# Two groups of the state-space stages at a time in the halves of TensorE's columns, and gate rows spread by DMA, in a two-layer hybrid backbone step

## The reference, cut to what matters

```python
def _adaln(cond, w, b):
    m = jax.nn.silu(cond) @ w + b          # w is 1024 x 3072
    return jnp.split(m[:, None, :], 3, axis=-1)     # shift, scale, gate

def _layer(x, mods, lp, ...):
    shift, scale, gate = mods
    h = _rmsnorm(x, lp['norm_g']) * (1.0 + scale) + shift
    z = h @ lp['w_in']                      # one projection feeds three mixers
    ...
    ya = _conformer_conv(conv_in, ...)      # A: depthwise conv, 31 taps, LayerNorm, silu
    yb = _s5_bidirectional(ssm_in, ...)     # B: 32 groups x 16 channels, 64 complex states
    o = _blocked_attention(q, k_all, v_all) # C: 8 heads, 2 KV heads, RMS-normed q and k
    ...
    mixed = g_a * br_a + g_b * br_b + g_c * br_c
    x = x + gate * (mixed @ lp['w_out'])
```

## Time and profile before

| | us |
|---|---|
| median of 3 runs | 691.57 |
| profiled execution | 691.89 |
| its span | 690.1 |
| PE busy | 643.8 (93%) |
| DVE busy | 535.7 (78%) |
| ACT busy | 309.6 (45%) |
| POOL busy | 80.4 (12%) |

### The profile page before, as it was taken

How to read it: one execution, slowest core, us unless ns; L and a number is a source line. 1 busy time by engine, 2 the same in 40 slices (tenths; PEclk the granted TensorE clock), 3 DMA queues, 4 the chain that set the end, 5 groups by cost and what they waited for, 6 DMA issues and landing times.

```text
span 690.1 us, 9683 instructions
## 1 busy us (share of the span) xinstructions
PE 643.8 (93%) x3573; PEld 460.7 (67%) x3573; DVE 535.7 (78%) x996; ACT 309.6 (45%) x534; POOL 80.4 (12%) x81
## 2 busy tenths in 40 slices
PE   3699799998999999999999899999999999989997
PEld 1377674554745688877887587465565578878885
DVE  2669889996676967789966837999767799987663
ACT  2665350540545354444546636044256544445441
POOL 2100220147000000010001710012700000010000
PEclk9999999999999999999999999999999999999999
DMA  7991817654583655655443337570443345655531
GB/s 263 373 315 58 264 60 230 238 186 119 174 284 120 180 160 173 183 162 153 162 149 113 116 137 267 179 258 29 151 151 106 106 127 184 199 163 181 184 102 61
DMA packets 67307, 117.66 MB, mean 171 GB/s; under 512 B 11052, under 2 KB 15484, under 8 KB 67260
## 3 DMA queue, kind: packets, MB, share of 16 engines
q1 hardware_dynamic: 66980, 116.94, 52.9%
q10 hardware_dynamic: 280, 0.11, 0.1%
HBM read 112.51 MB, written 1.38 MB: 165 GB/s over the span
## 4 chain that ended last, share of the span: by engine, by line
PE 72%; DVE 12%; SPq 6%; ACT 3%; issue 3%; DMA 2%; POOL 1%; ACTq 0%; POOLq 0%; DVEq 0%
PE proj L816 19%; PE proj L844 11%; PE proj L846 11%; PE proj L845 11%; PE side L831 4%; PE side L987 3%; PE side L974 2%; PE side L1068 2%; DVE raw_split L1506 2%; PE long L786 2%; PE side L1016 2%; SPq L629 1%; PE proj L786 1%; PE side L1066 1%; DMA raw<-in_w_in 1%
## 5 line engine op out<-in xcount | busy, mean ns | idle before, releaser
L816 PE MATMUL proj<-raw,hT 128*128 128x512 f32 (+1 forms) x320 | 132.0, 558 | 0.0
L1609 DVE SCALAR_TENSOR_TENSOR cvacc<-cvpad,taps,cvacc 128x256 f32<-128x256 f32 x240 | 99.0, 478 | 0.2
L816 PEld LDWEIGHTS proj<-raw,hT 128*128 128x128 f32 x320 | 58.2, 190 | 58.8 <-issue 57.0
L1212 ACT ACTIVATE wide_split<-raw 128x1024 fp32r<-128x1024 f32 x56 | 58.7, 1060 | 56.2 <-PE proj L846 56.2
L1506 DVE TENSOR_TENSOR raw_split<-raw,wide_split 128x1024 fp32r<-128x1024 f32 x56 | 67.8, 1221 | 17.2 <-ACT wide_split L1212 16.5
L845 PE MATMUL proj<-raw_split,H_split 128*128 128x512 f32 x192 | 75.5, 393 | 0.0
L844 PE MATMUL proj<-wide_split,H_split 128*128 128x512 f32 x144 | 57.9, 402 | 4.2 <-DVE raw_split L1506 4.2
L846 PE MATMUL proj<-wide_split,H_split 128*128 128x512 f32 x144 | 56.9, 395 | 0.0
L1212 ACT ACTIVATE utok_split<-raw 128x1024 fp32r<-128x1024 f32 x28 | 29.6, 1058 | 34.5 <-PE proj L846 34.5
L1506 DVE TENSOR_TENSOR raw_split<-raw,utok_split 128x1024 fp32r<-128x1024 f32 x28 | 34.2, 1221 | 12.3 <-ACT utok_split L1212 12.3
L2010 POOL TENSOR_SCALAR st<-st 128x1 f32<-128x1 f32 x8 | 4.6, 571 | 332.5 <-DVE st L1924 251.8
(11 more groups left out here) (255 smaller groups left out, 1377.6 us busy)
## 6 DMA issues: line engine op xcount, KB each, us to landing
raw<-in_w_in SPq DMA_DIRECT2D x104, 512.0 KB, 4.5
raw<-in_w_ada SPq DMA_DIRECT2D x48, 512.0 KB, 5.4
raw<-in_w_out SPq DMA_DIRECT2D x16, 512.0 KB, 3.8
raw<-in_w_ssm_glu SPq DMA_DIRECT2D x8, 512.0 KB, 7.1
raw<-in_w_ssm_out SPq DMA_DIRECT2D x8, 512.0 KB, 3.8
raw<-in_w_attn_out SPq DMA_DIRECT2D x8, 512.0 KB, 4.2
raw<-in_w_conv_out SPq DMA_DIRECT2D x8, 512.0 KB, 3.7
raw<-in_w_in SPq DMA_DIRECT2D x8, 256.0 KB, 3.6
```

The costliest lines, as they stand in the source:

```text
L816: m = T.matmul(proj.bank((l, u, s))[:, 0:n], lhs[:, s, kt, :], w[:, i, :], start=(kt == 0), stop=last)
L1212: S.activation(piece_room[m], piece_raw(m), ACT.Copy).then_inc(piece_hi, 1)
L1609: m = V.scalar_tensor_tensor(acc, src, taps[:, t, j:j + 1], acc, ALU.mult, ALU.add)
```

## The change

Five parts.

1. **K in pairs.** Groups g and g + 4 go alternately into output partitions 0 to 47 and 64 to 111, that is into the two halves of the array's columns, in 4 banks of 8 groups instead of 8 of 4. K 0 now stands ahead of unit kv, K 1 ahead of unit sg. ACT makes as many copies as before, four per bank.
2. **Y in pairs.** Group 4q + i and group 16 + 4q + i go alternately into partitions 0 to 63 and 64 to 127. ACT copies out 64 x 256 twice per quarter instead of 64 x 512 once.
3. **States.** All four quarters are copied right after the scan, quarters 2 and 3 into `tA` and `tB`, which are free then.
4. **Gates.** The PE matmuls of L1103, their ACT copies, the transposes `adaT` 2 and the bias addition on DVE go. In their place SP loads the gate's bias into rows of `taprow` at unit q (two DMAs, `bias_loads`), POOL adds it to the adaLN rows into `bz` after K 1 (`gaterow`, 128 x 256), and SP's `gate_rows`, ahead of the fourth slab of each wout, issues four DMAs of 128 KB: each reads one row of 256 numbers (1 KB) of one partition of `bz` 128 times and writes it to all 128 partitions of `th`. DVE waits for them (`gate_in`).
5. **Taps.** Ahead of Y 22 and 12 (layer 0 and 1) instead of 26 and 14; in Y 12 instead of 19; in B0 and B1 14 or 20 each instead of 12 or 18; what is left, at C0, is 20 and 24 instead of 13 and 19.

```diff
-TAPS_IN_ZONE = (26, 14)
-TAPS_IN_Y = (8, 5, 6)
+TAPS_IN_ZONE = (22, 12)
+TAPS_IN_Y = 12
-CONV_B = (12, 18)
+CONV_B = (14, 20)
...
+            + [("UT",), ("S",), ("cp",), ("bz", 0), ("convT", 0), ("convT", 1), ("unit", "q"), ("K", 0), ("unit", "kv"), ("bz", 1),
+               ("adaE", l, 2), ("sumsq", 0), ("sumsq", 1), ("K", 1), ("gaterow",), ("unit", "sg"), ("scan", 0, NCHUNK),
+               ("HY",), ("unit", "ag")] + nxt("adaE", n, 0)
+            + [("qkn",), ("conv", TAPS_IN_ZONE[l], None), ("Y",)] + nxt("adaT", n, 0)
...
+        states = [HY[:, 0], HY[:, 1]] + [t[:, :].rearrange("p (g r s k) -> p g r s k", g=8, r=2, s=NS) for t in (tA, tB)]
...
+            def gate_rows(l, h):
+                sp.wait_ge(gaterow_done, l + 1)
+                for s in range(NS):
+                    key = (l, "gate" + str(h), s)
+                    th_claim(sp, key)
+                    for i in range(2):
+                        row = P // ADA_TILES * (2 * h + i) + s
+                        sp.dma_start(th_view(key)[:, ADA_W * i:ADA_W * i + ADA_W],
+                                     gaterow[row:row + 1, :].unsqueeze(1).to_broadcast([1, P, ADA_W])).then_inc(gate_in, 16)
...
+                    if stg[0] == "wout" and i == 3:
+                        gate_rows(l, stg[1])
...
                         for b in range(4):
-                            g = 4 * i + b
                             for r in range(2):
-                                m = T.matmul(side.bank(key)[0:48, 80 * b:80 * b + 80], bz[:, r, g % 16, :],
-                                             CP[:, r, :, g, :], start=(r == 0), stop=(r == 1))
+                                for a in range(2):
+                                    g = 8 * i + 4 * a + b
+                                    m = T.matmul(side.bank(key)[64 * a:64 * a + 48, 80 * b:80 * b + 80], bz[:, r, g % 16, :],
+                                                 CP[:, r, :, g, :], start=(r == 0), stop=(r == 1))
...
-                        for gi in range(8):
-                            g = 8 * q + gi
-                            o = side.bank(key)[0:64, 64 * gi:64 * gi + 64]
-                            T.matmul(o, Uz[:, g, :], M[:, :, g // 2, :], start=True, stop=False)
+                        for i in range(4):
+                            gs = [4 * q + i, G // 2 + 4 * q + i]
+                            out = [side.bank(key)[64 * a:64 * a + 64, 64 * i:64 * i + 64] for a in range(2)]
+                            for a in range(2):
+                                T.matmul(out[a], Uz[:, gs[a], :], M[:, :, gs[a] // 2, :], start=True, stop=False)
                             for r in range(2):
-                                m = T.matmul(o, HY[:, q % 2, gi, r, :, :].rearrange("p s k -> p (s k)"),
-                                             CP[:, r, 1:L + 1, g, :], start=False, stop=(r == 1))
+                                for a in range(2):
+                                    m = T.matmul(out[a], states[q][:, 4 * a + i, r, :, :].rearrange("p s k -> p (s k)"),
+                                                 CP[:, r, 1:L + 1, gs[a], :], start=False, stop=(r == 1))
...
-                if k == "wout":
-                    h = stg[1]
-                    side.drained(pe, ("adaT", l, 2))
...
+                elif k == "gaterow":
...
+                    tt_(gaterow, adarow[part], biasrow, ALU.add).then_inc(gaterow_done, 1)
```

More of the change, by code:

```diff
@@ L192, in side_uses @@
     if k == "K":
-        return [(("K", l, 4 * stage[1] + i), 1) for i in range(4)]
+        return [(("K", l, 2 * stage[1] + i), 1) for i in range(2)]
     if k == "att":
@@ L213, in side_uses @@
     if k == "wout":
-        merged = [(("mixT", l, s, 1), 1) for s in range(NS)] if stage[1] == 0 else []
-        return [(("gate", l, stage[1], s), 1) for s in range(NS)] + merged
+        return [(("mixT", l, s, 1), 1) for s in range(NS)] if stage[1] == 0 else []
     return []
@@ L558, in build, with gates_in @@
         pool_chain = sem("pool_chain")
[L560 to L561 removed]
+        def gates_in(l, h, s):
+            return (gate_in, 32 * (4 * l + 2 * h + s + 1))
         def ls(l, s):
@@ L582, in build @@
             elif stg[0] == "wout":
-                th_list += [((l, "gate" + str(stg[1]), s), ("side", (u_gate(l, stg[1], s))),
+                th_list += [((l, "gate" + str(stg[1]), s), gates_in(l, stg[1], s),
                              ("proj", (l, "wo" + str(stg[1]), s))) for s in range(NS)]
@@ L600, in th_wait @@
                 proj.drained(eng, what[1])
-            elif what[0] == "side":
-                side.drained(eng, what[1])
             else:
@@ L617, in toeplitz @@
         def toeplitz(eng, l):
-            for i in range(5, 8):
+            for i in range(1, 4):
                 side.drained(eng, ("K", l, i))
@@ L980, in _ @@
                     pe.wait_ge(bz_done, 2 * l + half + 1)
-                    for i in range(4 * half, 4 * half + 4):
+                    for i in range(2 * half, 2 * half + 2):
                         key = ("K", l, i)
@@ L1094, in _ @@
                     m.then_inc(side.full, 1)
-                if k == "wout":
-                    h = stg[1]
-                    side.drained(pe, ("adaT", l, 2))
-                    for s in range(NS):
-                        key = ("gate", l, h, s)
-                        side.claim(pe, key)
-                        for i in range(4):
-                            col = ada[:, l, 2 * DT + 4 * h + i, s:s + 1]
-                            m = T.matmul(side.bank(key)[:, P * i:P * i + P], col.to_broadcast([P, P]), ident[:, :],
-                                         start=True, stop=True)
-                        m.then_inc(side.full, 1)
                 if k == "pass":
@@ L1398, in _ @@
                 elif k == "K":
-                    for i in range(4 * stg[1], 4 * stg[1] + 4):
+                    for i in range(2 * stg[1], 2 * stg[1] + 2):
                         key = ("K", l, i)
                         side.filled(act, key)
-                        src = side.bank(key)[0:48, 0:320].rearrange("p (g a i c) -> p a i g c", g=2, a=2, i=L + 1)
-                        for a in range(2):
-                            dst = KTs[:, :, a, 32 * i:32 * i + 32].rearrange("p i (g c) -> p i g c", g=2)
-                            m = S.activation(dst, src[:, a, :, :, :], ACT.Copy)
+                        for half in range(2):
+                            src = side.bank(key)[64 * half:64 * half + 48, 0:320].rearrange("p (g a i c) -> p a i g c",
+                                                                                           g=2, a=2, i=L + 1)
+                            g0 = 32 * (2 * i + half)
+                            for a in range(2):
+                                dst = KTs[:, :, a, g0:g0 + 32].rearrange("p i (g c) -> p i g c", g=2)
+                                m = S.activation(dst, src[:, a, :, :, :], ACT.Copy)
                         m.then_inc(side.freed(key), 1)
@@ L1478, in _ @@
                 elif k == "wout":
-                    h = stg[1]
-                    for s in range(NS):
-                        key, gk = (l, "gate" + str(h), s), ("gate", l, h, s)
-                        side.filled(act, gk)
-                        th_claim(act, key)
-                        S.activation(th_view(key), side.bank(gk)[:, :], ACT.Copy).then_inc(side.freed(gk), 1)
-                    if h == 0:
+                    if stg[1] == 0:
                         high_parts(piece_at[(l, "wo0", 0)] + len(wout_room))
@@ L1856, in _ @@
                     dve.wait_ge(scan_done, l + 1)
-                    for q in range(2):
+                    dve.wait_ge(cp_done, 2 * (l + 1))
+                    for q in range(4):
                         states_bwd(q)
@@ L1911, in _ @@
                 elif k == "Y":
-                    for q in range(2, 5):
-                        for _ in range(TAPS_IN_Y[q - 2]):
-                            conv_tap(*taps_left.pop(0))
-                        if q < 4:
-                            side.filled(dve, ("Y", l, q - 2))
-                            states_bwd(q)
+                    for _ in range(TAPS_IN_Y):
+                        conv_tap(*taps_left.pop(0))
                 elif k == "cback":
@@ L2059, in _ @@
                         k_norm(l, s)
+                elif k == "gaterow":
+                    part = ("ada", l, 2)
+                    side.filled(pool, ("K", l, 3))
+                    ada_ring(part).drained(pool, part)
+                    pool.wait_ge(bias_in, 32 * (l + 1))
+                    tt_(gaterow, adarow[part], biasrow, ALU.add).then_inc(gaterow_done, 1)
                 elif k == "bbar":
@@ L2084, in _ @@
                     if half:
-                        side.filled(pool, ("K", l, 3))
+                        side.filled(pool, ("K", l, 1))
                     else:
```

71 lines of the change are left out of this document (39 added, 32 removed).

## The result

The changed kernel took 709.69 us (median of 4 runs, 708.78 to 709.93) against 691.85 us for the kernel before in the same session: 1.0257 times as long, with a 95% interval of 1.0238 to 1.0275. It is slower by some 18 us; the forecast was slower by 35. The profiled execution has a span of 707.0 us (before: 690.1) at a mean granted clock of 0.959 (before: 0.989).

A forecast was written before the change was run, and what follows sets the result against it. PE, busy 93% of the span, was taken to bound the kernel. 691.9 - 8.5 (layer 0) - 6.0 (layer 1) + 2.8 (taps) + 47.2 (gate rows) = 727.4, as median 727.0 us; range 672 to 745, the forecast's own 715 to 745.

The forecast's parts named there:

- the rival of hidden rows: In wout, many engines read the one partition at once (363 GB/s), so PE never waits for gate rows: 674.9 us; chance 0.24.
- K, per half: K's matmuls in pairs at 81 ns: a half falls from 4.56 to 2.6 us, 1.9 less.
- zone of layer 0: K and Y in layer 0: pairs gain 3.8 us in K and 4.7 in Y, 8.5 together.
- zone of layer 1, with the wait for k: K and Y in layer 1: gain 7.7 us less 1.7 for the clock after PE's wait, 6.0 (4 to 9).
- taps in layer 1: Nine more taps in layer 1's B0, B1 and C0 lengthen DVE's work there: +2.8 us (0 to 3.6).
- gate rows, per layer: In wout, gate DMAs from one partition, 20.5 us a half, stand ahead of slabs in one queue: +23.6 us a layer, +47.2.
- the -2.5 of the gate matmuls: Gate matmuls removed from PE: -2.5 us a layer if gate rows are in time; the gate rows' cost takes its place.
- The pace plus 10 ns: Cost of a pair in K and Y: one record's pace plus 10 ns, 81 ns in K and 68 in Y.
- the last rival: Pairs in K and Y don't overlap, 121 ns each: 737 us with slow gate rows, 685 with hidden ones; chance 0.05.
- They need k's norm: Layer 1 after Y: the transposes of the sample's q wait for k's norm, due at 499.1 us; PE stands about 2.5 us.
- POOL gets through when DVE's taps stop: Layer 1: POOL's norm product ends with DVE's taps at 496.7 us, k's norm at 499.1.
- Slabs that pass the rows: In wout, later slab packets overtake the slow gate rows on the 16 rings, only DVE waits: 686 us; chance 0.06.

The follow-up runs named there:

- the gates alone: The kernel before with only the gate rows by DMA, K, Y, state copies and taps untouched: 723.51 us, ratio 1.0467.
- the halves in turn: The changed kernel with gate rows from 16 partitions, K and Y writing one column half of a bank wholly before the other: 679.61 us, ratio 0.9817.
- The version with fewer taps: The changed kernel with gate rows from 16 partitions, eight taps fewer ahead of layer 1's copy of k (`kz`): 666.61 us, ratio 0.963.
- the version with 16 sources: The changed kernel with each gate transfer reading 16 partitions 8 times each instead of one 128 times: 670.77 us, ratio 0.9718.
- the ladder: The kernel with 16-partition gate rows, each transfer now reading two or four partitions at chosen distances: one execution, 693.64 us.
- the last two experiments: Both on 16-partition gate rows, layer 1: eight taps fewer ahead of `kz`, 666.61 us; no taps in the zone ahead of Y, 668.06 us.

## Why the prediction was right or wrong

*The mechanism and the sign were right*: the gate rows, read from one partition, hold up the slabs, and that outweighs what the pairs gain. The size was twice too large, 35 us for 18: 709.7 us lies below the forecast's own range (715 to 745) and within 672 to 745 only because that one reaches to the rival of hidden rows.

Term by term, in us; what was measured comes from the matching places above:

| step | predicted | measured |
|---|---|---|
| K, per half | -1.9 | -2.2 |
| zone of layer 0 | -8.5 | -9.65 |
| zone of layer 1, with the wait for k | -6.0 | -6.1 |
| taps in layer 1 | +2.8 | +2.4 |
| gate matmuls ahead of wout, both layers | 0 | -3.3 |
| a half fall of the clock that did not come | 0 | -1.6 |
| merged transposes, both layers | 0 | +0.9 |
| gate rows, per layer | +23.6 | +17.0, +17.1 |

The K halves are part of the zones. Without that row the measured column adds up to the 16.8 us of the places.

**The step that was mis-sized** is "That is +23.6 a layer, +47.2"; it measured +17.0 and +17.1. Its parts: I took 20.5 us for a batch, between 4.8 and 5.8 a transfer. In the kernel with the gates alone, first issue to last landing takes 43.55 us (339.89 to 383.44) where I had 48.5. Take off five slabs at 1.3 (an estimate from the 400 GB/s at which they move) and each batch took 18.5, 4.6 a transfer, 28 GB/s. The upper end of the paths was nearer than the middle that I chose: the 109 GB/s of sixteen neighbours, four times 27, gave the right value, and 22.7, what one engine gets, was never a bound from below for many engines. That is 4 us of the 6.6 a layer. About one more is the start: the rows go out as soon as the third slab has been issued, at 339.9 and not 341.0, since they wait for no slot; and one more is the five slabs, for which my times had 7.5 us. The rest I did not trace.

**A wrong netting** comes on top. I wrote that the gate rows' cost takes the place of the -2.5 of the gate matmuls. The first gate block stands ahead of wout, and the gate rows are issued by PE's progress; so its 1.7 us a layer are kept. And the first wait in wout isn't the last slab, as I had it, but the second half of the merged product (`qM_split`, 7.7 us), since its place on DVE lies behind a slab of wo 0. It belongs to the same delay and changed nothing in the sum.

**The pairs.** The pace plus 10 ns was too careful: 60 ns a pair in Y, 73 in K, the pace itself. The case of the last rival (121 ns) was seen nowhere in K and Y, and the halves in turn show that it is the alternation that gains. That the strided weights make the 121 ns of the earlier trace rows stays a guess; no run changes them alone. The Trainium skill's rule that weight loads overlap matmuls in flight only when the row groups differ ("TensorE: Matmul & The Clock Gate", Part 3, The mechanism) is not what happens here: the matmuls of a pair use the same 128 rows, differ in columns alone, and run together (2.35 against 4.56 us a K half), with loads of 119 to 124 ns at 73 ns a pair.

**Layer 1.** The 6.0 came out at 6.1, but not for my reason. The steps that failed are "They need k's norm" and "POOL gets through when DVE's taps stop". POOL's norm ended at 497.3 us, 5.8 us before the taps did, and PE's transposes, from 498.5 on, had no wait for it. On the prediction's scale, from which the changed kernel lies 4.5 us behind at this place, that is 492.8 in place of 499.1 (the sum for the end of the taps, 493.36 and 3.2, gives 496.6 and not 496.7, which changes nothing). Its product took 0.52 us where it had taken 6.60, although DVE's taps had begun. So the rule that I leaned on, that this product ends with the taps, doesn't hold each time, and the runs don't show on what it depends. POOL and DVE around it in the changed kernel (start, us):

```profile
494.06 0.52 POOL L2016 TENSOR_TENSOR qk<-qk,qst 128x128 f32<-128x128 f32 x1
...
496.77 0.52 POOL L2016 TENSOR_TENSOR qk<-th 128x128 f32<-128x128 f32 x1
```

```profile
493.45 9.66 DVE L1623 SCALAR_TENSOR_TENSOR cvacc<-cvpad,taps,cvacc 128x256 f32<-128x256 f32 x22
503.14 0.64 DVE L1882 COPY kz<-side 64x128 f32<-64x128 f32 x2
```

What PE waits for is `kz`, DVE's own copy of k behind the 24 taps. I had asked who waits for k and not what is queued on DVE ahead of the next thing that PE needs. That the sum was right is luck: PE came to the end of Y with 11.8 us gained, where I had 10.2, and the wait for `kz` and the clock after it took 5.7 back, where I had 4.2 for k's norm. The version with fewer taps, 4.2 us faster, shows the cause.

**Layer 0.** The Toeplitz chain moved ahead with PE, as predicted, and PE waits 3.5 us for it rather than 2.2. In 233 to 239 us the kernel before had a clock of 0.72, and the changed one 1.00 at the same place, 1.6 us that no step of mine contains.

**The rivals.** Hidden rows (674.9) fell: 27 GB/s with 13 engines busy. The time is near that of the version with 16 sources (670.8), where the rows do pass quickly. Slabs that pass the rows fell too, and harder than I had argued: even from another queue they only trickle past the rows, at 6 GB/s beside POOL's queue and 28 to 81 beside ACT's.

## What to carry to other kernels

A transfer that spreads one partition over 128 was read at 27 GB/s here and kept 13 to 15 of the 16 DMA engines busy meanwhile, whichever of three queues it was on; make copies of the row in several partitions first, as a matmul gave them here for nothing. In the ladder partitions four apart did not share a path, two apart did. The small matmuls of K and Y, which use up to half of the array's columns, cost half once neighbours in the program wrote different halves; look then at once for what is queued on the other engines ahead of the next operand. When a change has several parts, price each apart: here +33 and -14 were one kernel that could be had at -20 to -25. And look up in the timeline where a wait stands before you build on its name in a list: the last two experiments rest in part on one that stood elsewhere.

## What the runs showed of the hardware that I had not expected

- DMA engines are shared by waiting packets, not by moved bytes: at 0.82 busy they moved 27 GB/s. Beside the rows of POOL's queue the slabs got next to nothing until the rows were nearly through, beside those of ACT's 28 and 81 GB/s.
- A packet of 1 KB took 46 ns with its path to itself, 84 ns when two engines read partitions two apart, and 0.50 us when 13 engines read one partition.
- An issue of a DMA can stall its engine: while packets of the gate rows were under way, three issues on ACT took 14.17 us, and ACT did nothing else. Two on POOL took 1.1 to 1.3 us.
- A transfer whose source has two or four partitions at the outside of its pattern ran on two or four engines (DMA share 0.14 for two); the one with a single source partition ran on 13. So the spread over 16 partitions gives both, engines and paths.
- Weight loads and matmuls of a pair in different column halves run together at 60 ns a pair with contiguous weights of 64 columns; another line, with strided weights, takes 121 ns.
